# Modulation in twelve blocks of 512 columns, queries projected chunk by chunk, tokens and weights loaded first

## The reference

```python
mod = jax.nn.silu(c) @ w_mod + b_mod          # once with c_ctx, once with c
shift1, scale1, gate1, shift2, scale2, gate2 = jnp.split(mod, N_MOD, axis=-1)
h = _rms_norm(x, g_pre_mix) * (1 + scale1) + shift1
q, k, v, gu, gv = jnp.split(h @ w_in, SPLITS, axis=-1)   # 512, 128, 128, 512, 512 columns
attn = ...   # context: softmax over context keys, with a sink; latents: rotary, window of 128, cached context keys
gm = gelu(gu) * (gm_ws @ norm(gelu(gv)) + gm_b)          # in chunks of 128 tokens
x = x + gate1 * _rms_norm(concat(attn, gm) @ w_out, g_post_mix)
h2 = _rms_norm(x, g_pre_ffn) * (1 + scale2) + shift2
x = x + gate2 * _rms_norm(moe(h2), g_post_ffn)           # 32 experts, top 1 of 4 groups, top 2 of 8
```

## Time and profile before

| | |
|---|---|
| median of 3 runs | 660.07 us (659.71 to 664.84) |
| the profiled execution | 659.92 us, its span 658.1 us |
| TensorE matmuls busy | 544.3 us (83%) |
| DVE, ACT, POOL busy | 188.8, 151.6, 175.6 us |
| transfers | 173.15 MB, mean 263 GB/s |
| chain that ended last | PE 46%, DMA 36%, DVE 7%, ACT 3% |

### The profile page before, as it was taken

How to read it: one execution, slowest core, us unless ns; L and a number is a source line. 1 busy time by engine, 2 the same in 40 slices (tenths; PEclk the granted TensorE clock), 3 DMA queues, 4 the chain that set the end, 5 groups by cost and what they waited for, 6 DMA issues and landing times.

```text
span 658.1 us, 9133 instructions
## 1 busy us (share of the span) xinstructions
PE 544.3 (83%) x3051; PEld 297.7 (45%) x3051; DVE 188.8 (29%) x571; ACT 151.6 (23%) x374; POOL 175.6 (27%) x242
## 2 busy tenths in 40 slices
PE   0479999999988788999997889899998778897700
PEld 0235654444445455455553446465654334454400
DVE  1150222001176765144447411111111111111027
ACT  1630102001106655122223011111111111111133
POOL 1000000002422433033334533343343222221204
PEclk9999999999997999999999899999999898899965
DMA  7999207136099500442146799999999999999368
GB/s 238 405 403 397 107 1 271 49 122 262 1 264 410 223 2 1 168 165 82 65 169 246 262 346 394 409 407 412 403 397 404 389 393 397 400 413 411 142 276 218
DMA packets 53935, 173.15 MB, mean 263 GB/s; under 512 B 7740, under 2 KB 8420, under 8 KB 52976
## 3 DMA queue, kind: packets, MB, share of 16 engines
q1 hardware_dynamic: 45680, 153.88, 60.9%
q0 software_dynamic: 7184, 15.70, 7.3%
q10 hardware_dynamic: 1008, 2.75, 1.0%
HBM read 163.75 MB, written 16.68 MB: 274 GB/s over the span
## 4 chain that ended last, share of the span: by engine, by line
PE 46%; DMA 36%; DVE 7%; SPq 3%; ACT 3%; issue 3%; POOL 1%; POOLq 0%; DVEq 0%; ACTq 0%
DMA ring<-in_w_down_dram 17%; PE ps L714 11%; PE ps L611 10%; PE ps L592 5%; PE ps L513 5%; DMA w<-in_w_down_dram 5%; DMA w_6d<-in_w_down_dram 4%; PE ps L531 3%; PE ps L593 3%; DMA w_7d<-in_w_down_dram 2%; PE ps L861 2%; DMA ring<-in_w_mod_dram 2%; PE ps L691 2%; DMA ring<-in_w_up_dram 2%; SPq L424 2%
## 5 line engine op out<-in xcount | busy, mean ns | idle before, releaser
L861 PE MATMUL ps<-ring,xt 128*64 128x256 f32 x704 | 84.1, 393 | 14.6 <-DMA ring<-in_w_up_dram 9.5
L861 PEld LDWEIGHTS ps<-ring,xt 128*64 128x64 f32 x704 | 55.7, 141 | 49.2 <-DMA ring<-in_w_up_dram 15.7
L611 PE MATMUL ps<-ring,h_t 128*128 128x512 f32 x160 | 69.5, 593 | 0.0
L1354 DVE TENSOR_TENSOR hid<-act_g,ps 128x128 f32<-128x128 f32 x32 | 9.2, 288 | 196.6 <-ACT act_g L1572 196.6
L861 PE MATMUL ps<-w,xt 128*64 128x256 f32 x416 | 51.5, 401 | 10.5 <-DMA w<-in_w_up_dram 7.5
L714 PE MATMUL ps<-ring,mix_t 128*128 128x512 f32 x120 | 53.6, 596 | 0.0
L1698 POOL DMA_INDIRECT expert_results<-y_sb,idx_out x32 | 32.8, 1024 | 59.0 <-ACT y_sb L1586 49.8
L861 PEld LDWEIGHTS ps<-w,xt 128*64 128x64 f32 x416 | 33.6, 144 | 32.7 <-DMA w<-in_w_up_dram 12.2
L611 PEld LDWEIGHTS ps<-ring,h_t 128*128 128x128 f32 x160 | 30.1, 190 | 37.6 <-issue 37.6
L592 PE MATMUL ps<-ring,h_t 128*128 128x512 f32 x80 | 42.0, 607 | 2.7 <-DVE h_t L1013 2.7
L1629 POOL TENSOR_TENSOR gm_stats<-gm_stats,half_pow 128x8 f32<-128x8 f32 x5 | 9.7, 1941 | 129.4 <-DVE gm_stats L1079 129.4
(11 more groups left out here) (239 smaller groups left out, 723.9 us busy)
## 6 DMA issues: line engine op xcount, KB each, us to landing
ring<-in_w_mod_dram SPq DMA_DIRECT2D x8, 3072.0 KB, 19.6
ring<-in_w_gate_dram SPq DMA_DIRECT2D x20, 1024.0 KB
ring<-in_w_up_dram SPq DMA_DIRECT2D x20, 1024.0 KB
ring<-in_w_down_dram SPq DMA_DIRECT2D x20, 1024.0 KB
w<-in_w_gate_dram SPq DMA_DIRECT2D x12, 1024.0 KB
w<-in_w_up_dram SPq DMA_DIRECT2D x12, 1024.0 KB
y_back<-expert_results SPq DMA_DIRECT2D x5, 1024.0 KB, 8.7
ring<-in_w_in_dram SPq DMA_DIRECT2D x2, 2048.0 KB, 17.7
```

The costliest lines, as they stand in the source:

```text
L611: last = pe.matmul(ps[:, 4 + u % 4, :], h_t[:, k, i * P:(i + 1) * P], w[:, k, :], start=(k == 0), stop=(k == KC - 1))
L861: last = pe.matmul(bank[fh * SLOT:(fh + 1) * SLOT, 0:FE].rearrange("p (a f) -> p a f", a=2), x_t[:, k % 4, (k // 4) * SLOT:(k // 4 + 1) * ...
```

## The change

- w_mod is taken in twelve blocks of 512 columns. `MB_FIRST` gives the order: the first half of shift1, the first half of scale1, then their second halves, then the rest. In a block each of the four column groups of the array takes another 128 of the block's columns, and runs over all eight chunks of features, so that the sum over features is complete in it. The copy to `part` is 128 columns wide, there is one transpose a block, and one DVE instruction adds the bias. Blocks alternate between two banks.
- The 96 KB of the ring are cut into six places of 16 KB for these items, and `PLACES` says which item goes where. SP loads x first, then m0, m1, half of the queries' weights, m2, m3, the other half, and kv; the later items wait as the diff shows.
- The constants, the conditions, the rows and the cached keys are issued from ACT's queue, and all are awaited together. POOL waits for the latent tokens before it issues the router's weights.
- Queries are projected chunk by chunk: for each chunk of 128 features all five tiles, into banks 3 to 7. The first four chunks need blocks 0 and 1 only; blocks 2 and 3 are computed between the chunks. Scale and shift are applied chunk by chunk. Keys and values follow, tile by tile, in banks 0 and 1.
- Blocks 4 and 5 stand where blocks 3 and 4 stood; blocks 6 to 9 follow the second gate projection, blocks 10 and 11 the spatial products.

```diff
...
+WIDE = 6
...
-MB = 768
+MB = 512
 N_MB = N_MOD * D // MB
 MB_CHUNKS = MB // P
+MB_FIRST = [0, 8, 4, 12] + list(range(16, N_MOD * KC, MB_CHUNKS))
...
+        wide = ring[:].rearrange("p r n -> p (r n)").rearrange("p (u n) -> p u n", n=KC * MB)
...
-        part = sb("part", [P, 2, MB], F32, t0)
+        part = sb("part", [P, 2, P], F32, t0 + 4 * KB)
...
+        PLACES = [["m0", "gu", "m8"], ["m1", "gv", "m9"], ["m2", "m4", "m10"], ["m3", "m5", "m11"],
+                  ["q", "m6"], ["kv", "m7", "wo"]]
+
+        def place(name):
+            return [u for u in range(WIDE) if name in PLACES[u]][0]
 
         def item(name):
-            r = ITEMS.index(name)
-            return ring[:, slot_of(r), :], ring_in[slot_of(r)], landed(r)
+            u = place(name)
+            if name == "wo":
+                return ring[:, RING - 1, :], wide_in[u], 16 * 2 + 16 * 5
+            return wide[:, u, :], wide_in[u], 16 * (PLACES[u].index(name) + 1)
 
         def weights(c):
...
+            def load_mod(b):
+                dst, done, _ = item(f"m{b}")
+                j = MB_FIRST[b] * P
+                sp.dma_start(dst.rearrange("p (k f) -> p k f", k=KC),
+                             w_mod[0, :, j:j + MB].rearrange("(p k) f -> p k f", k=KC)).then_inc(done, 16)
+
+            def load_in(name, a, n, ks, done):
+                sp.dma_start(item(name)[0][:, 0:KC * n].rearrange("p (k f) -> p k f", k=KC)[:, ks],
+                             w_in[0, :, a:a + n].rearrange("(k p) f -> p k f", p=P)[:, ks]).then_inc(done, 16)
+
+            every = slice(0, KC)
+            load_mod(0)
+            load_mod(1)
+            load_in("q", 0, ATT, slice(0, KC // 2), wide_in[place("q")])
+            load_mod(2)
+            load_mod(3)
+            load_in("q", 0, ATT, slice(KC // 2, KC), s_qkv)
+            load_in("kv", ATT, 2 * KVW, every, wide_in[place("kv")])
+            sp.wait_ge(mod_mm, 1)
+            load_in("gu", QKV, GM, every, wide_in[place("gu")])
+            sp.wait_ge(mod_mm, 2)
+            load_in("gv", QKV + GM, GM, every, wide_in[place("gv")])
+            sp.wait_ge(mod_mm, 3)
+            load_mod(4)
+            sp.wait_ge(mod_mm, 4)
+            load_mod(5)
+            sp.wait_ge(qkv_mm, 1)
+            load_mod(6)
+            sp.wait_ge(qkv_mm, TILES)
+            load_mod(7)
+            sp.wait_ge(mod_mm, 5)
+            load_mod(10)
+            sp.wait_ge(gu_mm, TILES)
+            load_mod(8)
+            sp.wait_ge(mod_mm, 6)
+            load_mod(11)
+            sp.wait_ge(gu_mm, 2 * TILES)
+            load_mod(9)
+            sp.wait_ge(mod_mm, 8)
+            dst, done, _ = item("wo")
...
-                s, v = USED[ITEMS[N_FIRST + j - RING]]
-                sp.wait_ge(s, v)
+                sp.wait_ge(mod_mm, 10 + j)
...
-                if b:
-                    pe.wait_ge(mod_part, b)
-                for hh in range(2):
-                    for k in range(KC):
-                        g = k % 4
-                        last = pe.matmul(ps[32 * g:32 * g + 32, hh, 0:MB // 2], cond[:, k, :],
-                                         w[:, k, hh * (MB // 2):(hh + 1) * (MB // 2)],
-                                         start=(k < 4), stop=(k >= 4))
+                if b >= 2:
+                    pe.wait_ge(mod_part, b - 1)
+                if b == 4:
+                    pe.wait_ge(kv_read, TILES)
+                for k in range(KC):
+                    for g in range(MB_CHUNKS):
+                        last = pe.matmul(ps[32 * g:32 * g + 32, b % 2, 0:P], cond[:, k, :],
+                                         w[:, k, g * P:(g + 1) * P], start=(k == 0), stop=(k == KC - 1))
                 last.then_inc(mod_mm, 1)
 
             def mod_turn(b):
                 pe.wait_ge(mod_part, b + 1)
                 if b:
                     pe.wait_ge(mod_col, b)
-                else:
-                    pe.wait_ge(s_cols, 1)
-                if b == 3:
+                if b == 4:
                     pe.wait_ge(qk_act, TILES)
-                    pe.wait_ge(qk_dve, TILES)
-                for j in range(MB_CHUNKS):
-                    last = transpose(ps[:, 2 + j // 4, (j % 4) * P:(j % 4 + 1) * P],
-                                     part[:, b % 2, j * P:(j + 1) * P])
-                last.then_inc(mod_tr, 1)
...
-                mod_block(b)
-                mod_turn(b)
-                for i in tiles:
-                    turn_tokens(i)
+            mod_block(0)
+            mod_turn(0)
+            for i in range(3):
+                turn_tokens(i)
+            mod_block(1)
+            for i in range(3, TILES):
+                turn_tokens(i)
+            mod_turn(1)
 
...
+            w_q = w_q.rearrange("p (k f) -> p k f", k=KC)
+            pe.wait_ge(s_cols, 1)
+
+            def queries(k, tiles):
+                if k % 4 < 2:
+                    pe.wait_ge(h_dve, 2 * (k // 4) + k % 4 + 1)
+                else:
+                    pe.wait_ge(h_act, 2 * (k // 4) + k % 4 - 1)
+                if k == 0:
+                    pe.wait_ge(q_in, q_v)
+                if k == KC // 2:
+                    pe.wait_ge(s_qkv, 16)
+                for i in tiles:
+                    pe.matmul(ps[:, 3 + i, 0:ATT], h_t[:, k, i * P:(i + 1) * P], w_q[:, k, :],
+                              start=(k == 0), stop=(k == KC - 1))
+
+            queries(0, range(TILES))
+            queries(1, range(TILES))
+            mod_block(2)
+            queries(2, range(TILES))
+            mod_turn(2)
+            mod_block(3)
+            queries(3, range(2))
+            mod_turn(3)
+            queries(3, range(2, TILES))
+            for k in range(4, KC):
+                queries(k, range(TILES))
+
+            w_kv, kv_in, kv_v = item("kv")
+            w_kv = w_kv[:, 0:KC * 2 * KVW].rearrange("p (k f) -> p k f", k=KC)
+            pe.wait_ge(kv_in, kv_v)
+            pe.wait_ge(mod_col, 4)
             for i in range(TILES):
-                if i < 2:
-                    pe.wait_ge(h_dve, i + 1)
-                    pe.wait_ge(h_act, i + 1)
-                else:
-                    pe.wait_ge(q_read, i - 1)
+                if i >= 2:
                     pe.wait_ge(kv_read, i - 1)
                 for k in range(KC):
-                    if i == 0 and k == 2:
-                        pe.wait_ge(s_qkv, 16)
-                    h = h_t[:, k, i * P:(i + 1) * P]
-                    pe.matmul(ps[:, 4 + 2 * (i % 2), 0:ATT], h, w[:, k, 0:ATT], start=(k == 0), stop=(k == KC - 1))
-                    last = pe.matmul(ps[:, 5 + 2 * (i % 2), 0:2 * KVW], h, w[:, k, ATT:QKV],
+                    last = pe.matmul(ps[:, i % 2, 0:2 * KVW], h_t[:, k, i * P:(i + 1) * P], w_kv[:, k, :],
                                      start=(k == 0), stop=(k == KC - 1))
                 last.then_inc(qkv_mm, 1)
                 if i:
...
-            mod_turn(3)
-            mod_block(4)
+            mod_turn(4)
+            mod_block(5)
 
             def spatial_weights():
 
-                mod_turn(4)
...
+            mod_block(6)
+            for b in range(7, 10):
                 mod_block(b)
-                mod_turn(b)
+                mod_turn(b - 1)
+            mod_turn(9)
 
 
...
                           gm_v[:, :, h * GMD:(h + 1) * GMD], start=True, stop=True).then_inc(gm_mm, 1)
-            mod_block(7)
+            mod_block(10)
+            mod_block(11)
             for i in range(TILES):
...
-                link(dve.tensor_reduce(mod[:, j0:j0 + MB_CHUNKS, :], both_banks[:, 0:MB_CHUNKS, 0:2, :], AX_X, ALU.add))
+                j0 = MB_FIRST[b]
                 bias = cols[:, ROWS["b_mod"][0] + j0:ROWS["b_mod"][0] + j0 + MB_CHUNKS]
-                dve.tensor_tensor(mod[:, j0:j0 + MB_CHUNKS, :], mod[:, j0:j0 + MB_CHUNKS, :],
+                dve.tensor_tensor(mod[:, j0:j0 + MB_CHUNKS, :],
...
+            def pre_mix_half(z):
+                ks = slice(4 * z, 4 * z + 4)
+                g = row("pre_mix")[:, ks].unsqueeze(2).broadcast_to((P, 4, 2))
+                dve.wait_ge(mod_col, 2 * z + 2)
+                dve.tensor_copy(pre[:, 0, 1, ks], mod[:, ks, :])
+                link(dve.scalar_tensor_tensor(pre[:, 0, 0, ks], mod[:, KC + 4 * z:KC + 4 * z + 4, :], 1.0, g,
+                                              ALU.add, ALU.mult))
+                dve.engine_nop().then_inc(s_pre, 1)
+                if z == 0:
+                    dve.wait_ge(ht_dve, TILES)
+                    dve.wait_ge(ht_act, TILES)
+                for k in range(4 * z, 4 * z + 2):
+                    for cn, (a, b) in enumerate(((0, P), (P, TILES * P))):
+                        last = dve.tensor_scalar(h_t[:, k, a:b], h_t[:, k, a:b], pre[:, 0, 0, k, cn:cn + 1],
+                                                 pre[:, 0, 1, k, cn:cn + 1], ALU.mult, ALU.add)
+                    last.then_inc(h_dve, 1)
+
+            mod_cols(0)
+            mod_sum(0)
+            for i in range(3):
+                tokens_out(i)
```

(36 more changed lines are left out.)

152 lines of the change are left out of this document (44 added, 108 removed).

## The result

The changed kernel takes 673.76 us (median of 4 runs, 671.57 to 674.57) against 659.89 us for the kernel before (4 runs): a ratio of 1.0187, with a 95% interval of 1.0133 to 1.0241. The forecast was 651.5 us with a range of 645 to 662. It was wrong in sign and outside its range. The profiled execution took 673.54 us; its span is 671.6 us, 13.5 more than before.

The account below looks back on a forecast made before the run. TensorE's work and waits before the first scores were taken to set when the weight-bound expert stream starts. From 659.92 us, -13.7 + 6.8 - 2.9 + 1.4 = -8.4 us gave 651.5 us, range 645 to 662.

Parts of the forecast that it names:

- Step 2: Kernel start: constants in at 12 us, first query product at 33.5 us instead of 47.23, a gain of 13.7 us.
- Rival (a): At the start, constants lose against bulk and land at 18 us, giving 6 us back: about 657.5 us; chance 0.15.
- Step 1: Modulation blocks: a new block takes 1.8 us instead of 2.72, its loads of weights hidden under matmuls.
- Rival (b): Modulation blocks do not hide their loads of weights, 3.8 us each: +20 us, 671.5 us in all; chance 0.13.
- Step 3: Start to gate projection: 55.7 us plus 3.8 for blocks 2 and 3 and 3.0 waiting for a write.
- Step 4: Gate projections: same matmuls with two cheaper blocks and turns, saving 2.9 us.
- Step 5: Last value matmul to first scores: six blocks instead of three, 21.5 us against 20.1, or +1.4.
- Rival (d): In front of the experts the gain is given back, their stream starting no earlier: 660 us; chance 0.05.
- the argument from the DMA share of 0.35 before the experts: From 262 to 345 us TensorE is always busy and transfers wait for it, so earlier gains arrive in full.

Follow-up runs that it names:

- The first experiment: The changed kernel with its eleven small loads back on SP's queue, ahead of the tokens; 662.98 us, ratio 1.0018 to the kernel before.
- both edits: The four repairs plus long records in blocks 6 to 11 and two filler products before the first query product; 656.54 us, ratio 0.9897 to the kernel before.
- the four repairs: Changed kernel: small loads on SP, 32-byte pieces, later wait for writes, block 9 behind spatial products; 661.45 and 661.97 us, ratios 0.9981 and 0.9958 to kernel before.

## Why the prediction was wrong

**Step 2 failed: the landing of the constants.** It put them at 12 us, between bounds of 9.1 and 14.6, and the start at 33.5. They landed at 24.3, the start was 48.03, and these 14.5 us are two thirds of the 22.0 us by which the profiled execution missed the forecast. The landing itself is 12.3 of them; the way from there to the first query product took 23.7 us where 21.5 were forecast. The upper bound came from one 64 KB write beside bulk, 7.6 us; measured were 13.34 us for the last 64 KB load, and 10.3 us even with the 32-byte pieces. The step also took the issue at about 7 us from SP, where it had been measured with nothing else queued; on ACT's queue, with the 4-byte pieces on the way, it was 10.96. Rival (a) had the right mechanism, "the constants lose against bulk", but with a landing at 18 us, a price of 6 us and a chance of 0.15. The first experiment, which changes only the queue and the place of these loads, brings the start to 35.73 us. That is 2.2 us from the forecast, of which the weights of block 0 are part: they were forecast at 16 to 18 us and the block started at 22.17.

The reason of the step, "ACT does nothing before 9 us, so their 6 us of issuing cost it nothing", was true and beside the point. What counted, as far as the runs tell, was not the time of the engine that issues but what is already in flight when the loads are issued, and that all three compute engines wait for the last of them. The Trainium skill, in "DMA: Bandwidth & Descriptors", section "Issuing engines are not separate DMA queues", says that transfers run on the same 16 engines and interleave, whichever engine starts them, and that a second issuer only saves issuing time. The runs agree: with the same pieces and otherwise the same kernel, the constants land at 8.2 us ahead of the bulk on one queue and at 15.2 beside it on a second one.

**Step 1 was right.** A block was forecast at 1.8 us and took 1.85 (3.70 us for two). Rival (b), slow blocks at 3.8 us, would have given almost the measured time (671.5) and is still refuted: the time came from elsewhere. With it falls, for this form of matmul, the rule of "TensorE: Matmul & The Clock Gate", Part 3, in the Trainium skill, that a load of weights overlaps only matmuls on other rows of the array. What step 1 did not see is that 64 records in 1.85 us use up the program three times as fast as 32 records in 2.72. That is in none of its sentences.

**Step 3 was right in its sum, in part by luck.** From the start to the gate projection 62.5 us were forecast and 62.35 measured, with a stall of 2.00 us instead of 3.0, because the write took 6.29 us and not 7.6, and 1.7 us of a low clock behind it (5.31 us for a tile of 3.62) that the step did not have. On the other side, the loss to the low clock behind the start, about 1.7 us, which step 2 left standing in the 55.7, did not come in this execution: its first 20 records took 8.82 us, at a granted clock of 1.00. The two cancel. Moving the wait took the stall away.

**Step 4 was right.** 74.3 us forecast, 74.5 measured.

**Step 5 was mis-sized: 21.5 us forecast, 27.5 measured.** Two terms are too small. Block 9 could start 11.4 us after the last value product (184.86 to 196.26) and not 7.4, which is 4.0 us: its weights took 11.27 us, where alone they take 9.18 and the output weights beside them cost another 1.6 to 2.1. And after the 3.02 us wait block 9 ran at the low clock, 1.8 us more. These make 5.8 of the 6.0 us. The late record of 1.90 us was not in the sum either, but here it lies under the wait for the weights; it costs time only where that wait is gone. It goes with the number of records and not with the weights: it stays when block 9 is moved or gets its weights sooner, and goes when the records are long.

**Rival (d) was wrong in the main**, and the argument from the DMA share of 0.35 before the experts held. Over the kernels here, what was won or lost at the scores shows in the span: 212.35 and 671.6 for the changed kernel, 199.23 and 659.1 with the constants on SP, 192.85 and 653.9 for the fastest. From the scores to the end of the span it is between 456.9 and 463.8 us in all of them. The five executions with scores before 198 us average 461.0 there and the four with scores after 204 us 458.9, so a small part of a gain may be given back; with one profile of each the scatter is too wide to tell.

**What remained open.** The kernel with both edits still needs 4.4 us more than before from the last value product to the scores, since it holds three blocks more there. Whether the output weights could come without slowing the others was not tried with the four repairs. Nor was it tried to hold the bulk back until small loads on ACT's queue have landed, which would tell the queue from the place in the order.

## What to carry to other kernels

Before loads are moved to an idle engine's queue, ask what is in flight when they are issued and who waits for the last of them: small loads that all engines need did best here ahead of the bulk, on the same queue, and in pieces as long as their layout allows. When an operation is cut into more and shorter instructions at the same total time, count the instructions per microsecond as well, and look for "issue" gaps inside a run of equal instructions. A reordering that starts work earlier is worth only what its new waits leave of it; sum the stretches one by one, as the 12.3 us here that left 3.3.

## What the hardware showed

- **Pieces of 4 bytes beside bulk.** Two loads of 4 KB each, in 1024 pieces, put in front on ACT's queue while SP's queue carried bulk, stretched the issue of the next small load to 5.84 us; with 32-byte pieces it was 0.51 us, and the last of the small loads landed at 15.7 us instead of 24.3. On one queue ahead of the bulk they cost less: the landing was at 8.7 us (7.8 to 8.2 with long pieces), and in the kernel before the issue of b_mod took 1.85 us (0.43 with long pieces).
- **TensorE seems to run out of instructions.** Gaps of 1.5 to 3.3 us without a releaser appeared inside the late runs of 64-record blocks in every kernel that had them, each with an instruction fetch just before it or at its start and the DMA engines at a share of 0.94 to 1.07. They sat at a fixed count of records, and four records of filler moved them by four. They were absent in the four executions with long records there: the kernel before, the same with 32-byte pieces, and the two with 16-record blocks. The Trainium skill, "Runtime: NRT & Kernel Launch", "Instruction fetch mechanics", says that instructions arrive in blocks of 16 KB and that the cost of crossing from one to the next is mostly hidden. The packets of these fetches have that size here (0.02 MB); the cost, if the gaps are theirs, was not hidden. That the fetch was late because the engines were full is only argued: the two were not separated.
- **The same 2 MB at different prices.** Block 9's weights took 9.18 us with the output weights held back (one execution) and 10.7 to 11.3 us beside them (four). In the later kernels, which have the output weights beside them too, it was 10.5 to 11.3 us with short records and 9.5 and 9.7 with long ones, so the price of sharing is not one number.
- **The clock after idle time.** The first 20 query records took 8.82 us (granted clock 1.00) in four executions and 10.5 us (granted clock 0.83 to 0.84) in six others, always behind the same 2.1 us of idle time; with 1.88 us of filler in that gap they took 8.85 in both kernels that had it. Since four came out fast without it, two executions make the filler's effect likely and do not prove it.
